# Second attention: the low part of the first output-projection weight item made by GpSimd in two halves, in place of VectorE at stage 0

## The reference, cut to what matters

```python
def swa_sink_mixer(h, cos, sin, k_band, v_band, w_q, w_out, sinks):
    ...
        m = jnp.maximum(s.max(-1, keepdims=True), sink)
        e = jnp.exp(s - m)
        p = e / (e.sum(-1, keepdims=True) + jnp.exp(sink - m))
        return jnp.einsum('bgrij,bjgd->bigrd', p.astype(vb.dtype), vb)
    ...
    return out @ w_out
```

## Time and profile before

| | |
|---|---|
| device time, median of 3 runs | 1342.18 us (1341.36 to 1342.96) |
| the profiled execution | 1342.56 us, its span 1340.8 us |
| PE busy | 1309.3 us (98%) |
| DVE, ACT busy | 396.7 us (30%), 281.1 us (21%) |
| POOL busy | 73.7 us (6%) |
| granted TensorE clock, mean | 0.995 |

### The profile page before, as it was taken

One profiled execution on the slowest core, in us unless ns is written; L12 is line 12 of the kernel. 1 busy time (PEld: TensorE's weight loads), 2 busy tenths in 40 slices (PEclk: granted clock), 3 DMA queues, 4 the chain that ended last, 5 costly groups with the idle time before them and its releaser, 6 DMA issues.

```text
span 1340.8 us, 31617 instructions
## 1 busy us (share of the span) xinstructions
PE 1309.3 (98%) x14080; PEld 792.6 (59%) x14080; DVE 396.7 (30%) x680; ACT 281.1 (21%) x510; POOL 73.7 (6%) x104
## 2 busy tenths in 40 slices
PE   8998999999999999999999999999999999999996
PEld 6765788888776544644744654564464474465444
DVE  6569576664576411001101101101100010120222
ACT  5465455544455200000010010000000001000001
POOL 2033300000012200000000000000000000000100
PEclk9999999999999999999999999999999999999998
DMA  9681268955542999999999999999999999999992
GB/s 321 197 220 64 86 196 292 360 182 202 147 153 66 381 397 420 417 395 420 418 395 419 419 406 390 420 418 393 420 417 372 419 418 396 407 419 418 418 420 104
DMA packets 115774, 443.16 MB, mean 331 GB/s; under 512 B 11936, under 2 KB 49088, under 8 KB 101312
## 3 DMA queue, kind: packets, MB, share of 16 engines
q1 hardware_dynamic: 108704, 423.39, 81.4%
q10 hardware_dynamic: 5792, 13.63, 2.8%
q0 software_dynamic: 1152, 4.19, 0.8%
HBM read 425.85 MB, written 15.34 MB: 329 GB/s over the span
## 4 chain that ended last, share of the span: by engine, by line
PE 94%; DVE 3%; ACT 2%; issue 1%; DMA 0%; DVEq 0%; ACTq 0%
PE bank L1677 43%; PE bank L1670 22%; PE bank L1537 6%; PE bank L1139 5%; PE bank L1141 5%; PE bank L1140 4%; PE bank L1539 3%; PE bank L1156 2%; PE bank L1413 1%; PE bank L1374 1%; ACT arena L945 1%; PE bank L1282 1%; PE bank L1169 1%; ACT wh L767 0%; PE bank L1462 0%
## 5 line engine op out<-in xcount | busy, mean ns | idle before, releaser
L1677 PE MATMUL bank<-ring,arena 128*32 128x448 f32 x2880 | 275.6, 539 | 0.7 <-issue 0.7
L2168 DVE TENSOR_TENSOR arena<-arena,bank 128x448 f32<-128x448 f32 x48 | 26.9, 616 | 728.0 <-PE bank L1677 728.0
L1677 PEld LDWEIGHTS bank<-ring,arena 128*32 128x32 f32 x2880 | 111.3, 110 | 156.8 <-issue 155.9
L1718 DVE TENSOR_TENSOR wl<-ring,wh 128x2048 fp32r<-128x2048 f32 (+1 forms) x55 | 124.1, 2259 | 57.6 <-ACT wh L767 57.3
L1670 PE MATMUL bank<-ring,arena 128*32 128x256 f32 x2304 | 126.0, 379 | 0.0
L1537 PE MATMUL bank<-hT,wh 128*128 128x512 f32 x344 | 121.6, 399 | 0.0
L767 ACT ACTIVATE wh<-ring 128x2048 fp32r<-128x2048 f32 (+1 forms) x56 | 105.5, 1888 | 34.9 <-PE bank L1141 32.3
L1677 PE MATMUL bank<-whs,arena 128*32 128x448 f32 x1152 | 111.6, 539 | 0.0
L1677 PE MATMUL bank<-wls,arena 128*32 128x448 f32 x1152 | 111.6, 539 | 0.0
L1670 PEld LDWEIGHTS bank<-ring,arena 128*32 128x32 f32 x2304 | 88.3, 110 | 38.6 <-issue 3.6
L1085 ACT ACTIVATE arena<-bank 128x448 f32<-128x448 f32 x48 | 22.6, 544 | 389.6 <-PE bank L1677 389.6
(11 more groups left out here) (287 smaller groups left out, 1304.0 us busy)
## 6 DMA issues: line engine op xcount, KB each, us to landing
ring<-in_moe_w_in_dram SPq DMA_DIRECT2D x120, 896.0 KB
ring<-in_moe_w_out_dram SPq DMA_DIRECT2D x48, 1024.0 KB
whs<-in_moe_w_in_dram SPq DMA_DIRECT2D x48, 896.0 KB, 17.8
wls<-in_moe_w_in_dram SPq DMA_DIRECT2D x48, 896.0 KB, 18.2
arena<-in_moe_w_in_dram SPq DMA_DIRECT2D x32, 896.0 KB, 15.7
whs<-in_moe_w_out_dram SPq DMA_DIRECT2D x24, 1024.0 KB, 21.4
wls<-in_moe_w_out_dram SPq DMA_DIRECT2D x24, 1024.0 KB, 22.3
ring<-in_dense_w_in_dram SPq DMA_DIRECT2D x22, 1024.0 KB
```

What stands on the lines that cost most here:

```text
L1677: ins = pe.matmul(bank[s + GROUPS * (kind == "u")][32 * j:32 * j + 32, 0:BLOCK], xgT[:, c, 32 * s:32 * s + 32], slot[:, BLOCK * j:BLOCK * ...
L1718: dve.tensor_tensor(wl[:, n % SPLITS, 0:size], slot_of(n)[:, 0:size], wh[:, n % SPLITS, 0:size].bitcast(F32), ALU.subtract).then_inc(split, 1)
L2168: ins = dve.tensor_tensor(act[:, s, :], act[:, s, :], bank[GROUPS + s][:, 0:BLOCK], ALU.mult)
```

## The change

The low part of item 57 is no longer made by DVE at stage 0. POOL makes columns 0 to 1023 of it after its work on job 1, and columns 1024 to 2047 after its work on job 5. At stage 10, DVE waits for both halves and then counts `split` up in POOL's place, so that the order of that semaphore stays as it was.

```diff
-ROUND_B, SPLIT_B = (0, len(JOBS_B) + 1, len(JOBS_B) + 2), (0, len(JOBS_B) + 1, len(JOBS_B) + 2)
+ROUND_B, SPLIT_B = (0, len(JOBS_B) + 1, len(JOBS_B) + 2), (len(JOBS_B) - 2, len(JOBS_B) + 1, len(JOBS_B) + 2)
+LOW_B = (1, 5)
...
+        low_made_b = sem("low_made_b")
...
                         ins.then_inc(normed, 1)
+                    if jobs is JOBS_B and i in LOW_B:
+                        n, cols = AT["out_b"], slice(1024 * LOW_B.index(i), 1024 * LOW_B.index(i) + 1024)
+                        pool.wait_ge(rounded, halved(n))
+                        pool.tensor_tensor(wl[:, n % SPLITS, cols], slot_of(n)[:, cols], wh[:, n % SPLITS, cols].bitcast(F32),
+                                           ALU.subtract).then_inc(low_made_b, 1)
...
             def attention(jobs, base, mbase, of_jobs, n_out, swa, heads, along):
                 at = SPLIT_B if swa else SPLIT_A
                 for i in range(len(jobs) + LAG_V + 1):
-                    if i in at:
+                    if swa and i == at[0]:
+                        dve.wait_ge(low_made_b, 2)
+                        dve.sem_inc(split, 1)
+                        n_split[0] = n_out + 1
+                    elif i in at:
                         split_weights(n_out + (1 if swa else 2) + at.index(i))
```

## The result

The changed kernel takes 1345.09 us (median of 18 runs, 1343.89 to 1346.49), the kernel before 1342.38 us (18 runs, 1341.36 to 1343.22): 2.7 us more, ratio 1.0019 with a 95% interval of 1.0013 to 1.0025. The forecast was no change, 1342.2 us, and its range ended at 1343.9. What came is the rival in which POOL holds DVE, which was worked out at 1344.8 us and given a chance of 0.10.

A forecast was written before the change was run, and what follows sets the result against it. DVE's first maximum was taken to wait for TensorE's scores, not the removed operation; -0.06 + 0.1 + 0 + 0 = +0.04 us on the profiled 1342.56, less 0.38 for the median, gave 1342.2 us, range 1340.6 to 1343.9.

The forecast's parts named there:

- the rival in which POOL holds DVE: Second attention: POOL's subtractions hold DVE's two-SBUF-input operations until done, 0.95 and 2.24 us; 1344.8 us, chance 0.10.
- What bounds the kernel, and the removal: Second attention's start: first maximum waits for TensorE's scores, so removing DVE's 2.29 us operation wins only 0.06 us.
- POOL's duration and gaps: After jobs 1 and 5: each half takes 2.34 us in POOL gaps of 5.10 and 5.55 us, cost nothing.
- Wait at stage 10, signal, SP: Stage 10: DVE's wait and increment hide in 0.28 us idle; expert item issued at some 410.3 us; cost 0 to 0.1.
- What the two engines do to each other, DVE's side: Small DVE operations beside POOL's halves: 0.1 us lost at the first half, 0 (0 to 0.1) at the second.

The follow-up runs named there:

- e1: Changed kernel with the low part of item 57 left out altogether, signal still given at stage 10; ratio to the kernel before 0.9995, stretch 49.24 us.
- e6: Changed kernel with POOL's first half made ahead of its work on job 0, second still after job 5; ratio to the kernel before 1.0021, stretch 51.01 us.
- e7: Changed kernel with both halves made on POOL ahead of its work on job 0; ratio to the kernel before 1.0016, stretch 50.99 us.
- e4: Changed kernel with each POOL half a multiplication by zero, one SBUF input instead of two; ratio to the kernel before 1.0001, stretch 49.72 us.
- e9: Changed kernel, first place only: POOL zero-fills columns 1024 to 2047, then multiplies columns 0 to 1023 by zero; one execution, 1341.84 us, stretch 49.64 us.
- e2: Changed kernel with POOL making the first half only, columns 1024 to 2047 left out; ratio to the kernel before 1.0007, stretch 50.11 us.
- e8: Changed kernel with each half made in four pieces of 256 columns, same places; ratio to the kernel before 1.0018, stretch 50.80 us.

## Why the prediction was wrong

By its own steps:

- *What bounds the kernel, and the removal.* Right. 0.06 us was forecast, 0.08 measured (e1). The chain's 2.29 us were not to be had, because the scores end 0.09 us ahead of the old start of the maximum.
- *POOL's duration and gaps.* Right: 2.34 us forecast, 2.40 and 2.35 measured; POOL was not late (3.58 and 4.99 us of idle time left).
- *Wait at stage 10, signal, SP.* Right: nothing in e1. The expert item was issued at 413.37 us, which the forecast had at 410.3 plus what the kernel lost by then, and TensorE waits for none of it.
- *What the two engines do to each other, DVE's side.* **This step failed.** It took 0.1 us lost at the first half and 0 at the second; measured were 0.87 and 1.80 us. The delays of 0.06 and 0.10 us were taken as the size of the effect, but they came from scalings of 256 columns with one input, about 0.91 us each. POOL's row of 391.81 is four of them, which start at 391.81, 392.71, 393.61 and 394.52; the operations at 393.84 and 394.78 came 0.23 and 0.26 us behind such a start and met only the last part of a short hold (the one at 393.84 ended at 394.10, 0.49 us behind 393.61). The row at 101.12 us, taken as the proof that a running POOL operation doesn't hold DVE, lay 1.56 us behind the start of POOL's one-input operation of 99.56, which took 1.83 us, so 0.27 us ahead of its end. None of the three rows could have shown a hold by a two-input operation. The prediction said so itself ("no row shows POOL with two inputs beside DVE") and still gave this case a tenth of the chance.

  The trace of the kernel before even has a DVE operation that is held to the end of a running POOL operation, at the routing; the prediction used that POOL operation for its duration only the earlier trace rows. POOL's and DVE's rows, and DVE's of the same operation in e6:

```profile
446.42 5.37 POOL L722 TENSOR_SCALAR pre<-h 128x2048 f32<-128x2048 f32 x1 [27.29 <-DVE h L2027]
450.44 1.37 DVE L2126 TENSOR_SCALAR selb<-lg 128x8 bf16<-128x8 f32 x1
```

```profile
454.12 0.23 DVE L2143 TENSOR_SCALAR selb<-lg 128x8 bf16<-128x8 f32 x1
```

  DVE's operation on eight columns ends at 451.81 us, POOL's at 446.42 + 5.37 = 451.79. In e6 it comes 0.10 us behind the end of POOL's (448.66 + 5.36 = 454.02) and takes 0.23 us.
- *The rival.* Its working held almost to the letter: holds of 0.95 and 2.24 us were worked out, 0.85 (1.07 less 0.22) and 2.08 (2.24 less 0.16) measured; a total of 2.6 us, 2.53 measured in the stretch; 1344.8 us, 1345.09 measured. Even the two lines that would be held were named. The range left it out by 0.9 us.

The Trainium skill's page "SBUF — State Buffer", section "Who interferes with whom", which the prediction weighed against the rows, says that the loser blocks fully for the other's whole instruction. For POOL's two-input subtraction the trace now agrees, with 2.24 us for a four-column operation, and for the memset, which the page leaves free, with 0.16 for the same operation. For one-input work beside a two-input operation of DVE the measurement differs: 1.05 to 1.12 of 2.77 us.

No experiment beats the kernel before beyond what can be measured. The most that can be won here is e1's 0.08 us, with the work left out altogether; a place for both halves in which they meet no two-input operation of DVE ahead of TensorE's need at stage 12 wasn't found. The free stretch at the start holds one half only (e6, e7); other places for the second half, such as right ahead of POOL's work on job 4, were not tried.

## What to carry to other kernels

An idle engine is no free engine if its reads can hold the full one. Ahead of moving work with two SBUF inputs from VectorE to GpSimd, list VectorE's operations with two SBUF inputs in the gap where the work would go, and price the one that meets a GpSimd operation at the rest of that operation, whatever its own size (four columns: 2.24 us); then take off what the idle time behind it takes in. A row clears a mechanism only if it has the same number of operands and falls at the same point of the other's operation; where no row has, the mechanism belongs in the range. And an operation that the chain names is worth only the time until its successor's next condition is met, here 0.08 us out of 2.29.

## What the runs showed of the hardware that was not expected

- A POOL operation with one SBUF input holds a DVE TENSOR_TENSOR with two SBUF inputs only in its first part: until 1.05 and 1.12 us behind its start at 1024 columns, out of 2.77 us (e4, e9), and until 0.49 us at 256 columns, out of 0.92 (line 1939 at 393.84 us in the kernel before; line 1950 at 414.55 in the changed one, which ended at 414.96, behind a scaling that started at 414.47). A memset held neither operation that it met.
- Not every operation of DVE gets off so lightly: the eight-column TENSOR_SCALAR of the rows above came 4.02 us behind the start of a one-input POOL operation and was held to its end. In the other runs that have the meeting it is the same (in e2 it ends at 450.10 + 1.37 = 451.47, POOL's operation at 446.07 + 5.36 = 451.43). Why it is held so long and line 1790 in e4 isn't, no run here shows.
- The other way round, POOL lost little here: its halves took 2.40 and 2.35 us, and the pieces of e8 2.84 us at the first place and 3.23 at the second. There the third piece, which started at 407.88 beside line 1986 of DVE, took 1.17 us, the first 0.73.
- The runs of one kernel lie on levels: e6 has 1343.0 to 1343.1, 1344.4 to 1344.8 and 1346.0 to 1346.2 us. Two places in the profiled executions explain a loss of this size, and both lie outside of the stretch. The first is in layer 0. TensorE's busy time and clock (us, PE busy (x), PEclk, DMA, GB/s), first of e2, then of the kernel before:

```profile
120.00:130.00 10.00, 6.69 (x55) 1.00 0.32 105
130.00:140.00 10.00, 8.79 (x67) 1.00 0.01 2
```

```profile
120.00:130.00 10.00, 6.68 (x53) 0.92 0.32 105
130.00:140.00 10.00, 10.00 (x59) 0.74 0.01 3
```

TensorE was busy 6.69 and 6.68 us in 120 to 130 us; the clock fell to 0.50, the lower of the two levels, in the kernel before and not in e2; the rounding of item 57 then starts at 384.95 instead of 383.82 us. The changed kernel has 0.83 in 10 to 20 us and again in 130 to 140 us, and its rounding starts at 385.58: this is where its 0.63 us comes from. So the kernel before was profiled on its upper level (1342.56 us, where its lowest run has 1341.36), and e2 on its lowest (1342.20 us).

The second place is the routing behind the attention, first of e6, then of the kernel before:

```profile
448.00:449.00 1.00, 0.99 (x7) 0.93 0.96 401
449.00:450.00 1.00, 1.00 (x5) 0.50 1.02 430
451.00:452.00 1.00, 1.00 (x17) 0.50 0.97 409
452.00:453.00 1.00, 1.00 (x7) 0.86 1.00 418
```

```profile
449.00:450.00 1.00, 1.00 (x7) 1.00 0.99 416
451.00:452.00 1.00, 1.00 (x10) 1.00 1.03 385
```

For some 3.4 us, worked out from these rows, the granted clock was 0.50, after TensorE had waited 1.36 us for DVE's layer norm. From the layer norm's start to the first expert matmul e6 takes 461.09 - 436.52 = 24.57 us, the kernel before 457.57 - 434.27 = 23.30: 1.27 us, about the distance of two levels. The kernel before and the changed one wait 1.36 us at the same place too and kept their clock there in their profiled executions; which of the other runs do is not told by a trace. The profiled executions of e6 to e8 had both losses (spans of 1344.3, 1344.3 and 1344.1 us). In e6 and e7 the highest level also came more often: 4 and 3 of 10 runs at 1346.0 us or more, 2 of 18 of the changed kernel. This would make their medians lie near the changed kernel's, though their stretches are 0.8 to 1.05 us shorter, but no trace counts the losses run by run; the lowest runs of e6 and e7 are 0.89 and 1.05 us below its lowest, that of e8 only 0.38. Differences below a microsecond were read from the stretch, not from the medians.
